# Two more turns through device memory in a float32 decoder trunk: differential keys and stick-breaking rows

## The reference, cut to what matters

```python
h = rms_norm(x, attn_norm[layer])
proj = h @ w_in                      # (256, 7428), split into
# u_pool | dq dk dv | sq sk sv | fq fk fv | f_logit | g_logit
q = rope(rms_norm(dq per half head, q_gain)); k = rope(rms_norm(dk ..., k_gain))   # differential attention
z = sq @ sk.T * HEAD_DIM ** -0.5     # stick-breaking: weights = sigmoid(z) * prod of later (1 - sigmoid(z))
# merged = sum over four branches of sigmoid(gate) * (branch output @ w_branch rows)
x = x + merged @ w_out
x = x + swiglu(rms_norm(x, ffn_norm[layer]), w_up, w_down)
```

## Time and profile before

| what | value |
|---|---|
| median of 3 runs | 835.85 us (835.82 to 836.11) |
| the profiled execution's own time | 836.77 us |
| its span, first to last instruction | 835.0 us |
| PE, PEld, DVE, ACT, POOL busy | 829.1, 685.4, 632.1, 443.2, 119.1 us |
| granted TensorE clock, mean over the span | 1.000 |
| bytes moved by DMA | 185.05 MB, mean 222 GB/s |

### The profile page before, as it was taken

One profiled execution on the slowest core, in us unless ns is written; L12 is line 12 of the kernel. 1 busy time (PEld: TensorE's weight loads), 2 busy tenths in 40 slices (PEclk: granted clock), 3 DMA queues, 4 the chain that ended last, 5 costly groups with the idle time before them and its releaser, 6 DMA issues.

```text
span 835.0 us, 11052 instructions
## 1 busy us (share of the span) xinstructions
PE 829.1 (99%) x4006; PEld 685.4 (82%) x4006; DVE 632.1 (76%) x934; ACT 443.2 (53%) x642; POOL 119.1 (14%) x89
## 2 busy tenths in 40 slices
PE   9999999999999999999999999999999999999998
PEld 8888788788888888888888888887888888888787
DVE  7898998899677666565679979977986866666653
ACT  6666755653554544544365576566543644444441
POOL 0651201018101000000005602010361000000000
PEclk9999999999999999999999999999999999999999
DMA  9867788687657766666766577886875576766751
GB/s 339 286 210 230 230 280 260 220 279 227 209 182 251 219 201 214 202 211 217 249 196 189 171 215 243 260 278 210 274 238 198 151 246 195 201 207 211 228 187 51
DMA packets 116055, 185.05 MB, mean 222 GB/s; under 512 B 18721, under 2 KB 40225, under 8 KB 116001
## 3 DMA queue, kind: packets, MB, share of 16 engines
q1 hardware_dynamic: 115568, 183.69, 69.5%
q10 hardware_dynamic: 432, 0.66, 0.3%
HBM read 168.05 MB, written 10.49 MB: 214 GB/s over the span
## 4 chain that ended last, share of the span: by engine, by line
PE 85%; DVE 9%; ACT 2%; issue 2%; DMA 1%; POOL 1%; ACTq 0%; DVEq 0%; SPq 0%
PE bulk L1854 27%; PE bulk L1855 26%; PE bulk L1858 26%; DVE w_lo L1158 3%; DVE wide L1467 1%; PE bankAB L1638 1%; DMA probs_diff<-wide 1%; POOL wide L831 1%; PE bulk L1910 1%; ACT w_hi L868 0%; PE bulk L1901 0%; PE bulk L1882 0%; PE bulk L1888 0%; ACT wide L1054 0%; ACT sb L1029 0%
## 5 line engine op out<-in xcount | busy, mean ns | idle before, releaser
L1158 DVE TENSOR_TENSOR w_lo<-raw,w_hi 128x1024 fp32r<-128x1024 f32 (+1 forms) x288 | 364.2, 1286 | 83.7 <-ACT w_hi L868 81.7
L868 ACT ACTIVATE w_hi<-raw 128x1024 fp32r<-128x1024 f32 (+1 forms) x286 | 295.1, 1047 | 210.8 <-PE bulk L1858 205.7
L1854 PE MATMUL bulk<-w_hi,hT_hi 128*128 128x512 f32 (+1 forms) x880 | 342.4, 389 | 1.2 <-DVE wide L1467 1.2
L1855 PE MATMUL bulk<-w_lo,hT_hi 128*128 128x512 f32 (+1 forms) x880 | 339.2, 385 | 0.0
L1858 PE MATMUL bulk<-w_hi,hT_lo 128*128 128x512 f32 (+1 forms) x880 | 336.2, 386 | 0.0
L1854 PEld LDWEIGHTS bulk<-w_hi,hT_hi 128*128 128x128 f32 x880 | 165.2, 188 | 35.2 <-DVE w_lo L1158 2.0
L1858 PEld LDWEIGHTS bulk<-w_hi,hT_lo 128*128 128x128 f32 x880 | 165.0, 188 | 33.2
L1855 PEld LDWEIGHTS bulk<-w_lo,hT_hi 128*128 128x128 f32 x880 | 165.3, 188 | 32.1
L1854 PE MATMUL bulk<-w_hi,aT_hi 128*128 128x512 f32 x174 | 67.8, 390 | 0.5 <-DVE wide L1503 0.5
L1858 PE MATMUL bulk<-w_hi,aT_lo 128*128 128x512 f32 x174 | 67.7, 389 | 0.0
L1855 PE MATMUL bulk<-w_lo,aT_hi 128*128 128x512 f32 x174 | 67.7, 389 | 0.0
(11 more groups left out here) (235 smaller groups left out, 704.4 us busy)
## 6 DMA issues: line engine op xcount, KB each, us to landing
raw<-in_w_in_dram SPq DMA_DIRECT2D x110, 512.0 KB, 4.8
raw<-in_w_ffn_up_dram SPq DMA_DIRECT2D x80, 512.0 KB, 4.2
raw<-in_w_ffn_down_dram SPq DMA_DIRECT2D x44, 512.0 KB, 3.7
raw<-in_w_branch_dram SPq DMA_DIRECT2D x20, 512.0 KB, 4.8
raw<-in_w_out_dram SPq DMA_DIRECT2D x16, 512.0 KB, 3.4
wide<-wide SPq DMA_DIRECT2D x160, 32.0 KB, 2.7
bias<-in_b_gate_dram SPq DMA_DIRECT2D x16, 256.0 KB, 4.5
raw<-in_w_ffn_up_dram SPq DMA_DIRECT2D x16, 256.0 KB, 3.2
```

The costliest lines, as they stand in the source:

```text
L868: act.activation(w_hi[:, g % RING, :, 0:width], raw[:, g % RAW, :, 0:width], ACT.Copy).then_inc(hi_ready, 1)
L1158: vec.tensor_tensor(w_lo[:, g % RING, :, 0:width], raw[:, g % RAW, :, 0:width], w_hi[:, g % RING, :, 0:width].bitcast(F32), ALU.subtract). ...
L1854: pe.matmul(dst, hi, whi, start=(k == ks[0]), stop=False)
L1855: pe.matmul(dst, hi, wlo, start=False, stop=False)
```

## The change

The items `dk` and `ss` change places. `dk` is squared and then copied from its bank by ACT into the SBUF tile where DVE norms it; its bank is free after that copy. `ss` is copied from its bank into `fox_gained`. Both are turned through device memory, and `tr_qk` and `tr_ss` are gone. The scale of 1/8 on the stick-breaking scores moves into the sigmoids. The conversion of the masks goes from DVE to ACT. The timetables and the SP slots of the transfers move.

```diff
 ITEMS = [
     ("dq", "w_in", [(OFF["dq"], 512)], KD),
+    ("dk", "w_in", [(OFF["dk"], 512)], KD),
     ("ss", "w_in", [(OFF["sq"], 512)], KD),
-    ("dk", "w_in", [(OFF["dk"], 512)], KD),
...
 MIXING_PE = [
-    (9, "tr_ss"), (14, "sb_scores", 0), (20, "sb_scores", 1), (24, "tr_qk", "dk"), (25, "scores", "diff", 0),
+    (21, "sb_scores", 0), (22, "sb_scores", 1), (25, "scores", "diff", 0), (30, "sb_out", 0), (30, "scores", "diff", 1),
...
-TURN_AT = {"dq": 16, "fox": 33, "diff": 48, "merged": 62}
+TURN_AT = {"ss": 13, "dq": 15, "dk": 18, "fox": 33, "diff": 48, "merged": 62}
-ROWS_AT = {"dq": (20, 21), ...
+ROWS_AT = {"ss": (17, 18), "dq": (19, 20), "dk": (22, 23), ...
-PROBS_AT = {("sb", 0): (23, 24), ...
+PROBS_AT = {("sb", 0): (26, 27), ...
 MIXING_ACT = [
-    (4, "qk_norm", "dq"), (8, "ss"), (10, "ss_evac"), (11, "lambda_sums"), (14, "qk_norm", "dk"), (14, "sb_breaks", 0),
-    (19, "svfq"), (21, "fkfv"), (22, "sb_breaks", 1), (23, "qk_evac", "dq"), (24, "qk_evac", "dk"), (25, "dv"),
+    (4, "qk_norm", "dq"), (8, "qk_norm", "dk"), (11, "lambda_sums"), (12, "ss"), (18, "ss_evac"), (19, "svfq"),
+    (21, "sb_breaks", 0), (21, "fkfv"), (22, "qk_evac", "dq"), (23, "qk_evac", "dk"), (23, "sb_breaks", 1), (25, "dv"),
 MIXING_DVE = [
-    (3, "qk_sums", "dq"), (5, "row_mean"), (5, "qk_norm", "dq"), (7, "lambda_sums"), (7, "ss_evac"), (10, "lambdas"),
-    (14, "qk_norm", "dk"), (16, "turn", "dq"), (19, "sb_weights", 0), (19, "sb_turn", 0), (23, "qk_evac", "dq"),
-    (24, "qk_evac", "dk"), (24, "sb_weights", 1), (24, "sb_turn", 1), (25, "maxima", "diff", 0), (27, "softmax", "diff", 0),
+    (3, "qk_sums", "dq"), (5, "row_mean"), (5, "qk_norm", "dq"), (7, "lambda_sums"), (12, "qk_norm", "dk"), (13, "turn", "ss"),
+    (15, "turn", "dq"), (18, "turn", "dk"), (18, "ss_evac"), (19, "lambdas"), (22, "qk_evac", "dq"), (22, "sb_weights", 0),
+    (22, "sb_turn", 0), (23, "qk_evac", "dk"), (24, "sb_weights", 1), (24, "sb_turn", 1), (25, "maxima", "diff", 0),
...
-                "dq": (normed, ("dq", t)), "pf": (u_ready, t), "dk": (normed, ("dk", t)), "ss": (ss_staged, t),
+                "dq": (normed, ("dq", t)), "pf": (u_ready, t), "dk": (dk_staged, t), "ss": (ss_staged, t),
...
             def qk_norm(layer, which):
                 if which == "dk":
-                    act.wait_ge(stage_done, nth(stage_done, layer, ("tr_ss", 1)))
+                    act.wait_ge(normed, nth(normed, layer, ("dq", 1)))
                 head_squares(layer, which)
+                if which == "dk":
+                    for t in range(TT):
+                        act.activation(xn("dk", t), item_bank(layer, ITEM_AT["dk"], t), ACT.Copy).then_inc(dk_staged, 1)
...
             def qk_evac(layer, which):
+                wait_spread(act, layer, which)
+                if which == "dk":
+                    act.wait_ge(stage_done, nth(stage_done, layer, ("sb_scores", 1)))
...
             def ss_evac(layer):
-                for t in range(TT):
-                    act.wait_ge(stage_done, nth(stage_done, layer, ("tr_ss", t)))
-                    src = bank["TO"[t]].rearrange("p (k q) -> p k q", k=4)
-                    act.activation(sT[0][:, 0:2, t * P:(t + 1) * P], src[:, 0:2, :], ACT.Copy, scale=HD ** -0.5)
-                    act.activation(sT[0][:, 2:4, t * P:(t + 1) * P], src[:, 2:4, :], ACT.Copy).then_inc(sT_hi, 1)
+                wait_spread(act, layer, "ss")
+                for t in range(TT):
+                    act.activation(by_quads(sT[0], (0, 4), t), spread_columns("ss", t, (0, 4)), ACT.Copy).then_inc(sT_hi, 1)
```

More of the change, by code:

```diff
@@ L233 @@
[L233 to L237, removed]
@@ new lines @@
+    (22, "sb_turn", 0), (23, "qk_evac", "dk"), (24, "sb_weights", 1), (24, "sb_turn", 1), (25, "maxima", "diff", 0),
+    (27, "softmax", "diff", 0), (27, "probs_turn", "diff", 0), (29, "pf"), (29, "fox_norm"), (29, "fox_forget"),
+    (30, "maxima", "diff", 1), (31, "sb_evac", 0), (32, "softmax", "diff", 1), (32, "probs_turn", "diff", 1),
+    (32, "sb_evac", 1), (32, "gate", 0), (32, "cum_evac"), (33, "maxima", "diff", 2), (33, "turn", "fox"),
+    (36, "pv_evac", "diff", 0), (36, "gate", 1), (37, "softmax", "diff", 2), (37, "probs_turn", "diff", 2),
@@ new lines @@
+    (37, "maxima", "diff", 3), (39, "softmax", "diff", 3), (39, "probs_turn", "diff", 3), (39, "fox_evac", "fq"),
+    (39, "fox_evac", "fk"), (40, "gate", 2), (41, "pv_evac", "diff", 1), (41, "maxima", "fox", 0), (41, "softmax", "fox", 0),
+    (41, "probs_turn", "fox", 0), (44, "pv_evac", "diff", 2), (44, "gate", 3), (45, "pv_evac", "diff", 3), (46, "diff_norm"),
+    (46, "turn", "diff"), (47, "maxima", "fox", 1), (48, "softmax", "fox", 1), (48, "probs_turn", "fox", 1), (49, "gate", 4),
+    (49, "pool_evac_b"), (52, "gate", 5), (55, "diff_evac", 1), (55, "diff_evac", 0), (56, "gate", 6),
@@ L244, in evacuations @@
+    (57, "pv_evac", "fox", 0), (57, "pv_evac", "fox", 1), (63, "turn", "merged"), (69, "merged_evac", 0), (69, "gate", 7),
+    (71, "merged_evac", 1)]
 def evacuations(mixing, *branches):
@@ L1124, in _ @@
                 layer, u = divmod(g, U)
+                if g == MASKS_AT:
+                    act.wait_ge(consts_loaded, 16)
+                    for i, name in enumerate(("ident", "causal", "strict_neg")):
+                        last = act.activation(masks[:, i, :], c(name), ACT.Copy)
+                    last.then_inc(masks_ready, 1)
                 for stage, *args in ACT_TIMETABLE.get(u, ()):
@@ L1354, in qk_evac @@
                     high, low = (by_quads(part, (0, 4), t) for part in qT[which])
[L1355 to L1359, removed]
+                    vec.tensor_tensor(low, spread_columns(which, t, (0, 4)), high.bitcast(F32), ALU.subtract).then_inc(qkT_ready, 1)
             def fox_evac(layer, which):
@@ L1372, in ss_evac @@
                     vec.wait_ge(sT_hi, nth(sT_hi, layer, t))
[L1373 to L1377, removed]
+                    vec.tensor_tensor(by_quads(sT[1], (0, 4), t), spread_columns("ss", t, (0, 4)), by_quads(sT[0], (0, 4), t).bitcast(F32),
                                       ALU.subtract).then_inc(sT_ready, 1)
@@ L1587, in _ @@
                 layer, u = divmod(g, U)
-                if g == FIRST["dk"]:
+                if g == FIRST["ss"]:
                     vec.wait_ge(consts_loaded, 16)
[L1590 to L1593, removed]
                 for stage, *args in DVE_TIMETABLE.get(u, ()):
@@ L1648, in tr_norm @@
                 ins.then_inc(stage_done, 1)
-            def tr_qk(layer, which):
-                for t in range(TT):
-                    pe.wait_ge(rotated, nth(rotated, layer, (which, t)))
-                    name = QK_BANKS[which][t]
-                    take(name, qkT_ready, layer, (which, t))
-                    for k in range(4):
-                        ins = pe.transpose(bank[name][:, k * P:(k + 1) * P], xn(which, t)[:, k * P:(k + 1) * P], identity)
-                    ins.then_inc(stage_done, 1)
             def tr_forget(layer):
@@ L1667, in tr_forget @@
                 ins.then_inc(stage_done, 1)
-            def tr_ss(layer):
-                for t in range(TT):
-                    pe.wait_ge(ss_staged, nth(ss_staged, layer, t))
-                    take("TO"[t], sT_ready, layer, t)
-                    for k in range(4):
-                        ins = pe.transpose(bank["TO"[t]][:, k * P:(k + 1) * P], scratch(t, SQ)[:, k * P:(k + 1) * P], identity)
-                    ins.then_inc(stage_done, 1)
             def cum(layer):
```

55 lines of the change are left out of this document (22 added, 33 removed).

## The result

The changed kernel takes **847.89 us** (median of 4 executions, 846.72 to 848.82) against 835.98 (4 executions) for the kernel before: the ratio is 1.014, 95% interval 1.0128 to 1.0152. It is slower by 11.9 us, where 7.5 were forecast and 847.0 was the upper end of the range. The profiled execution's own time is 847.44 us, its span 845.6, 10.6 more than before.

A forecast was written before the change was run, and what follows sets the result against it. The prediction took a DVE chain without slack from slot 24 to a PE gate item as the bound. Later first maxima, 3.5 + 2.0, and late dv, 1.0 + 1.0, added 7.5 us to 835.85: 843.3 us, range 834.5 to 847.

The forecast's parts named there:

- what bounds the kernel: From slot 24 to a gate item in each layer, a DVE chain without slack; PE arrives 0.6 us too early.
- The new wait: PE waits at unit 20 for ACT's svfq squares, queued behind the evacuation of ss: 3.2 and 1.7 us.
- R2: Rival, faster: the DVE chain has unseen slack and PE's sum decides; 832 to 833 us, chance 0.20.
- R1: Rival: the rows of ss land in time, so no wait; 838.0 us, chance 0.20 with cases near it.
- The landing of `ss`: Rows of ss back from device memory at 61.3 us, and 472.6 in the second layer.
- What DVE does ahead of it: Five subtractions to 41.4 us, dk's norm of 5.1, then further work until 51.7; 463.0 in the second layer.
- T + 17.7: DVE's first maximum comes 17.7 us after T: 86.1 and 497.4 us, later by 3.5 and 2.0.
- `dv` behind it: ACT's dv waits for pair 0's stick-breaking weights to be written out, another 1.0 us in each layer.
- R3: Rival: after a PE gap the clock falls, 3 to 5 us more, 847 to 850 us; chance 0.10.
- T: Start of PE's unit 21, forecast at 68.4 us in the first layer and 479.7 in the second.
- The clock leaving 1.0: Sign that the prediction is wrong: PE's granted clock does not stay at 1.0.
- A late `dq` or `dk` trip is hidden: Costs nothing: the keys' rows land by T + 7 and DVE reaches them only at T + 10.5.

The follow-up runs named there:

- the last pair of runs: extra_at_22 and extra_at_50: the kernel before with eight extra PE transposes in each layer, at two different places; 837.89 and 836.50 us.
- extra_at_22: Kernel before the change plus eight unused transposes on PE ahead of unit 22 of each layer; 837.89 us, ratio 1.0024.
- extra_at_50: Kernel before the change plus eight unused transposes on PE ahead of unit 50 of each layer; 836.50 us, ratio 1.0005.
- keys_only_early: keys_only with SP writing out dk's rows before it waits for dq's, dk's transfers having their own semaphores; 834.57 us, ratio 0.9977.
- fill_gap: Changed kernel plus 24 idle 128-column matmuls on PE ahead of unit 20, results unused; 846.56 us, ratio 1.012.
- breaks_first: svfq_first with the second pair's sigmoids on ACT moved ahead of the copy of dk's returned rows; 845.40 us, ratio 1.0108.
- svfq_first: Changed kernel with ACT doing svfq, which releases unit 20's bank, ahead of the evacuation of ss; 845.43 us, ratio 1.011.
- sticks_early: Kernel before the change, ss still second, but its rows turned through device memory instead of on PE; 835.91 us, ratio 0.9999.
- keys_only: Changed kernel with only dk's trip through memory kept; stick-breaking rows turned on PE, scores at 16 and 20; 836.30 us, ratio 1.0003.
- dk_out_early: breaks_first with SP writing out dk's rows before it waits for dq's, dk's transfers having their own semaphores; 850.07 us, ratio 1.0166.
- sticks_only: Changed kernel with only the trip of ss through memory kept; keys turned on PE at slot 20; 846.82 us, ratio 1.0134.

## Why the prediction was right and wrong

**Right: what bounds the kernel, and the direction.** The bound is shown by the last pair of runs. The new wait, its engine, its place and its releaser came as written. Rival R2, that PE's sum decides because the chain has slack, is refuted by the gate waits: unchanged in `extra_at_22`, gone in `extra_at_50` at a price of 0.4 us instead of 1.7. The cost of `extra_at_22` alone would fit R2 as well. R2 has a part in it that `keys_only_early` bears out: for a gain of more than 1.7 us in a layer the chain waits for PE. R1, no wait, is refuted by the profile after.

**The landing of `ss`: right to 0.6 us.** 61.88 against 61.3; in the second layer 481.12, of which 7.4 are the first layer's shift, so 473.7 against 472.6. The write-out took 5.1 us, 5.0 being taken from `rows_diff`. What DVE does ahead of it came out right partly by luck. In the first layer the five subtractions ended at 40.2 us and not at 41.4, and the norm of `dk` took 7.2 us (40.18 to 47.38) instead of 5.1. I had called POOL idle there, and it rotated until 44.2. In the second layer, where POOL had ended, the norm took 5.1. PE's waits of 3.74 and 2.65 against 3.2 and 1.7 (0.5 and 0.9 too small) follow from that.

**T + 17.7: right in the first layer.** From unit 21 (71.44) to the first maximum (89.15) it is 17.71 us. In the second it is 18.14, because there the copy of the keys waited 3.72 us for `rows_dk`. `dv` behind it cost 0.8 and 0.4 us instead of 1.0.

**The step that failed is the choice between the forecast and R3.** I took the clock as a rival with a chance of 0.10 and put it at nothing in the sum, though the forecast itself held a gap of 3.2 us. Nothing in the rows spoke for that: in the trace of before PE is never idle for longer than 1 us. The two belonged together. The gap of 3.74 put unit 20 on the lower level: 2.3 us by `fill_gap`, and T came at 71.44 and not 68.4 (3.0, of it 0.6 the landing).

Up to the second gate the profile has 4.0 us more than forecast (11.5 against 7.5). The clock's 2.3 is the greater part, the later landings are 0.6 and 1.1, the wait for `dk` in the second layer 0.4, and the cheaper `dv` gives 0.8 back; that makes 3.6, and 0.4 I can't place. The medians differ by 11.9, 0.4 more than the gates, which I can't place either. R3's price (3 to 5 us in all) was high for the one event it became. The measured time lies in R3's interval, 847 to 850, but that is more than R3's own sum gives (843.3 and 3 to 5 make 846.3 to 848.3), and it came about with one fall of the clock and 1.7 us of other misses. The clock leaving 1.0 had been named as a sign of being wrong.

The Trainium skill, "TensorE: Matmul & The Clock Gate", section "Why this matters for your kernels", asks that PE have no long idle gaps between bursts of matmuls. The first layer's 3.74 us with the fall near their end agree, and so does the clock of 1.00 behind the second layer's 2.65; the falls behind waits of 2.98 us (`breaks_first`) and 1.73 (`fill_gap`) don't follow from it.

**"A late `dq` or `dk` trip is hidden" held for a reason that the prediction didn't give.** It held in the first layer because DVE and ACT were 3 us late themselves. `svfq_first` took that delay away and the trip of `dk` stood there with 8.04 us. I had put the landing of the keys at T + 7 and left out a delay of SP. It waits in order for `dq`'s rows, and three loads collect behind the wait. `dk`'s write-out is issued behind these and takes 6.4 us up to the issue of its reads (67.50 to 73.87). The landing near 78.8 is T + 7.4 only because T was late as well.

**What the change costs, as shown.** It isn't the trip through memory by itself (`sticks_early`), nor the keys, nor that the stick-breaking rows are the third item (`keys_only`, where they are turned on PE). It is the third place and the trip together: rows that are ready late and then travel for 9 to 10 us. Their scores, two pairs of sigmoids, two rounds of weights and the write-out before `dv` now all lie in slots 18 to 28, in one series with the landings of three trips. Each wait that was taken away from that series (`svfq_first`, `breaks_first`) uncovered the next, and `dk_out_early` made one trip early at the cost of another: from 2.5 us less than the changed kernel to 2.2 us more. That a version with the sticks third could be brought to the time of before was not shown, and not tried further.

## What to carry to other kernels

When a forecast itself contains an idle gap of PE longer than any in the trace of before, price it with the lower clock behind it as well as without: here 2.3 us for a gap of 3.74. When one of several waits in a row of in-order stages is removed, work out the landing of the next transfer before pricing the gain; here 6.4 us of waits at unit 20 came back as 10.3 at slot 25. And whether a round trip through memory is free isn't a matter of its length: 11.8 us cost nothing where the scores were due 7.7 us after the rows had come back, and 9.4 us cost some 11 where they came back 0.6 us after PE had come to a unit whose bank was freed behind them. Look first at when the rows are ready, and at what else is queued behind them.

## What the runs showed of the hardware

- The clock's fall doesn't go by the length of the last gap alone. The granted clock was at 0.50 already when waits of PE of 3.74 (changed kernel), 5.16 (`breaks_first`), 6.10 (`svfq_first`), 6.61 and 6.88 us (`dk_out_early`) ended. It fell with PE busy again, 0.2 to 1.6 us behind the wait, after 4.25 (`svfq_first`), 3.12 (`sticks_only`), 2.98 (`breaks_first`) and 1.73 us (`fill_gap`). It stayed at 1.00 after 2.65 (changed kernel) and 2.68 (`fill_gap`).
- A write-out of 512 KB to device memory took, from its issue to its landing, 5.1 us for `ss` in the changed kernel and 6.3, 6.4 and 7.5 for `dk` (`keys_only`, changed kernel, `svfq_first`), where `dq`'s four reads and three loads had left in the 3.3 us ahead of it. Issued ahead of `dq`'s reads it took 2.6 (`keys_only_early`) and 4.2 (`dk_out_early`, with loads closely ahead). But in the first layer of `sticks_early` the write of `ss` took 6.8 with only loads ahead of it on SP's queue. Which of the two, reads or loads, makes a write slow was not taken apart.
- Four reads of 128 KB each had landed 8.0 us after the first was issued when another round trip was under way (`dk_out_early`, 65.49 to 73.47), and 4.2 us for `ss` in the changed kernel (57.63 to 61.88).
